# First conditioning vector from four 2 MB transfers, with x transposed meanwhile and kept in SBUF

## The reference

```python
c_act = jax.nn.silu(c)                                   # (1, 1024)
for i in range(2):
    mod = (c_act @ ada_w[i] + ada_b[i])[:, None, :]      # ada_w[i]: 1024 x 6144
    sh1, sc1, g1, sh2, sc2, g2 = jnp.split(mod, 6, axis=-1)
    u = x * (1.0 + sc1) + sh1                            # x: 1024 x 1024
    y = diff_attention(u, ...)                           # layer 0: q, k, v = u @ w_qkv, 8 heads
    x = _layer_norm(ALPHA * x + (1.0 + g1) * y, ...)     # the residual is ALPHA * x
    ...                                                  # MLP, again with a residual
```

## Time and profile before

| | us |
|---|---|
| three runs | 3074.52, 3080.66, 3080.73 (median 3080.66) |
| the profiled execution | 3074.19 |
| span of its trace | 3072.5 |
| busy: PE / PEld / DVE / ACT / POOL | 2708.4 / 2231.9 / 1689.0 / 1184.6 / 336.0 |
| mean granted TensorE clock | 0.949 of full speed |
| last conditioning block added | 75.1 |
| first product of head 0 starts | 111.6 |
| first scores of head 0 | 146.3 |

### The profile page before, as it was taken

One profiled execution on the slowest core, in us unless ns is written; L12 is line 12 of the kernel. 1 busy time (PEld: TensorE's weight loads), 2 busy tenths in 40 slices (PEclk: granted clock), 3 DMA queues, 4 the chain that ended last, 5 costly groups with the idle time before them and its releaser, 6 DMA issues.

```text
span 3072.5 us, 37975 instructions
## 1 busy us (share of the span) xinstructions
PE 2708.4 (88%) x12716; PEld 2231.9 (73%) x12716; DVE 1689.0 (55%) x2888; ACT 1184.6 (39%) x2125; POOL 336.0 (11%) x362
## 2 busy tenths in 40 slices
PE   1678878887999999999998788888789999999996
PEld 1566666665778888888776677777567888888884
DVE  3466666665575444354375777777558323232346
ACT  0355555554262120312255565665426212131223
POOL 2000000000020001016032322222101000000000
PEclk9789998886999999999999999999899999999997
DMA  6422222223434324142233111111353211111122
GB/s 195 143 68 73 70 69 66 64 59 145 150 95 130 103 69 135 44 129 61 71 115 86 21 32 27 27 32 26 128 159 86 77 48 48 48 48 48 48 82 76
DMA packets 331200, 245.78 MB, mean 80 GB/s; under 512 B 41000, under 2 KB 303447, under 8 KB 331103
## 3 DMA queue, kind: packets, MB, share of 16 engines
q1 hardware_dynamic: 314062, 185.82, 20.7%
q0 software_dynamic: 17040, 58.73, 6.3%
HBM read 215.12 MB, written 33.59 MB: 81 GB/s over the span
## 4 chain that ended last, share of the span: by engine, by line
PE 63%; DVE 13%; ACT 10%; issue 9%; DMA 4%; ACTq 0%; DVEq 0%; POOL 0%; SPq 0%; POOLq 0%
PE PA L1651 31%; PE SC L1651 24%; PE VB L1739 3%; DVE H L1184 2%; DVE soft L1566 2%; ACT H L729 2%; ACT X L745 2%; DMA ada<-in_ada_w 1%; DVE W L1102 1%; ACT X L1028 1%; ACT W L683 1%; PE TB L1658 1%; DVE H L1223 1%; ACT H L723 1%; DVE X L1588 1%
## 5 line engine op out<-in xcount | busy, mean ns | idle before, releaser
L1651 PE MATMUL PA<-U,W 128*128 128x512 f32 x3840 | 948.8, 402 | 80.8 <-DVE W L1102 46.9
L1651 PEld LDWEIGHTS PA<-U,W 128*128 128x128 f32 x3840 | 730.6, 192 | 245.5 <-issue 57.7
L683 ACT ACTIVATE W<-raw 128x1024 fp32r<-128x1024 f32 (+2 forms) x262 | 259.8, 992 | 830.9 <-PE PA L1651 389.9
L1651 PE MATMUL SC<-U,W 128*128 128x512 f32 x2064 | 484.2, 394 | 4.4 <-DVE W L1102 4.2
L1651 PEld LDWEIGHTS SC<-U,W 128*128 128x128 f32 x2064 | 389.5, 189 | 91.5 <-DVE W L1102 5.9
L1102 DVE TENSOR_TENSOR W<-raw,W 128x1024 fp32r<-128x1024 f32 (+2 forms) x262 | 313.8, 1198 | 99.6 <-ACT W L683 97.9
L1651 PE MATMUL PA<-H,W 128*128 128x512 f32 x1536 | 358.7, 393 | 3.2 <-DVE W L1102 3.2
L1651 PE MATMUL SC<-H,W 128*128 128x512 f32 x1536 | 354.4, 390 | 0.0
L1651 PEld LDWEIGHTS PA<-H,W 128*128 128x128 f32 x1536 | 288.6, 189 | 64.3 <-DVE W L1102 3.6
L1651 PEld LDWEIGHTS SC<-H,W 128*128 128x128 f32 x1536 | 288.5, 188 | 60.5 <-issue 1.0
L729 ACT ACTIVATE H<-TB 128x512 fp32r<-128x512 f32 (+3 forms) x216 | 107.8, 499 | 217.0 <-PE TB L1658 215.6
(11 more groups left out here) (209 smaller groups left out, 2984.1 us busy)
## 6 DMA issues: line engine op xcount, KB each, us to landing
raw<-in_ffn_w SPq DMA_DIRECT2D x160, 512.0 KB, 4.1
ada<-in_ada_w POOLq DMA_DIRECT2D x96, 512.0 KB, 4.7
U<-attention_out SPq DMA_DIRECT2D x4, 3584.0 KB, 17.4
raw<-in_da_w_qkv SPq DMA_DIRECT2D x24, 512.0 KB, 4.2
attention_out<-ostage SPq DMA_DIRECT2D x32, 256.0 KB, 2.7
raw<-in_da_w_o SPq DMA_DIRECT2D x16, 512.0 KB, 4.1
X<-residual SPq DMA_DIRECT2D x4, 2048.0 KB, 11.6
attention_out<-ostage SPq DMA_DIRECT2D x64, 128.0 KB, 2.3
```

The costliest lines, as they stand in the source:

```text
L683: nc.scalar.activation(W[:, slot, 0, 0:kt * P], raw[:, slot, 0:kt * P], ACT.Copy).then_inc(w_hi, 1)
L1651: ins = mm(bank, W[:, slot, a, kt * P:(kt + 1) * P], moving(b, kt)[:, cols], start=kt == first and (a, b) == SPLIT[0], stop=kt == last and ...
```

## The change

1. Scratch that lies under tensors not yet in use: `xin` (x by rows, 32 KB a partition) and `brow` (the bias table) lie where `U` will be, `ada0` (64 KB a partition) where `H` will be. So nothing of `x` waits for the bias table any more.
2. `ada_w[0][:, 0:2048]` comes in four transfers of 2 MB, issued by ACT as its first instructions, each with rows of 8 KB. DVE makes eight products of 128x2048 into `acc0` (the place of `ada`); PE adds over the partitions with 16 products after the last of them, DVE adds the bias vector once.
3. PE transposes `x` as soon as it has landed. ACT scales each half tile into `X[:, t]` (ALPHA * x), and SP stores the residual from there, in eight transfers of 512 KB.
4. ACT makes `U[:, 0]` straight from `X` with scale (1 + sc1) / ALPHA and bias sh1; DVE makes `u` from `X` in `tmp` and subtracts. The order of the half tiles is now half 0 of all t, then half 1.
5. Pieces 0 and 1 of head 0 are multiplied tile by tile as `x_lo` counts up, and `split_hi`/`split_lo` of slab 1 come earlier: `split_lo` of slabs 0 and 1 stands in DVE's program between the fifth and the sixth of the eight products.
6. POOL waits for the four transfers before it spreads the bias table, and loads the bias of head 0 (into `X[:, 4]`) only when all of `x_lo` is done.

```diff
+        with nc.sbuf_tensor("x_rows", [P, KT, S], F32) as xin, nc.sbuf_tensor("bias_row", [P, KT * S], F32) as brow:
+            pass
         U = sb("U", [P, 2, KT, S], F32R)
         X = sb("X", [P, KT, S])
+        with nc.sbuf_tensor("ada_first", [P, KT, 2 * S], F32) as ada0:
+            pass
         H = sb("H", [P, 16 * S], F32R)
...
@@ sync
             x_rows(0)
+            x_rows(1)
...
             sp.dma_start(bias_d, bvec).then_inc(bvec_out, 16)
-            sp.wait_ge(bvec_out, 16)
-            x_rows(1)
-
-            for n in range(KT * NH):
-                t, hf = n // NH, n % NH
-                sp.wait_ge(x_z, n + 1)
-                sp.dma_start(z_d[t, :, hf * HALF:(hf + 1) * HALF], tmp[:, 2 + n % 2, :]).then_inc(z_out[n % 2], 16)
+            for t in range(KT):
+                sp.wait_ge(x_z, NH * (t + 1))
+                sp.dma_start(z_d[t, :, :], X[:, t, :]).then_inc(z_out, 16)
@@ gpsimd
-            ada_loads(0, 0, 0)
-            with pool.Fori(1, 4) as b:
-                ada_loads(0, b, b)
+            for u in range(KT // 2):
+                pool.wait_ge(ada0_in[u], 16)
...
-            pool.wait_ge(xt, KT * NH)
+            pool.wait_ge(z_out, 16 * KT)
+            pool.wait_ge(x_lo, KT * NH)
             bias_load(0, 0, 0)
@@ scalar
+            for u in range(KT // 2):
+                act.dma_start(ada0[:, 2 * u:2 * u + 2, :],
+                              ada_w[0].rearrange("(t p) n -> p t n", p=P)[:, 2 * u:2 * u + 2, 0:2 * S]).then_inc(ada0_in[u], 16)
...
-            split_hi(0, 0, KT, None, 0)
             for n in range(KT * NH):
...
                 act.wait_ge(xt, n + 1)
-                act.wait_ge(x_u, n + 1)
-                nc.scalar.activation(U[:, 0, t, cols], tmp[:, n % 2, :], ACT.Copy).then_inc(x_hi, 1)
-                if n >= 2:
-                    act.wait_ge(z_out[n % 2], 16 * (n // 2))
-                nc.scalar.activation(tmp[:, 2 + n % 2, :], bank[:, 0:HALF], ACT.Copy, scale=ALPHA).then_inc(x_z, 1)
+                nc.scalar.activation(X[:, t, half(hf)], dense_bank[n % 4], ACT.Copy, scale=ALPHA).then_inc(x_z, 1)
+            split_hi(0, 0, KT, None, 0)
+            split_hi(1, 0, KT, None, 0)
+
+            act.wait_ge(aff_set, 1)
+            for n in range(KT * NH):
+                t, hf = n % KT, n // KT
+                nc.scalar.activation(U[:, 0, t, half(hf)], X[:, t, half(hf)], ACT.Identity, scale=aff[:, A_G, t:t + 1],
+                                     bias=modv(0, 0)[:, t:t + 1]).then_inc(x_hi, 1)
@@ vector
             for t in range(KT):
-                ada_mac(0, t)
-            mod_add(0, block_cols(0, 0))
-            with dve.Fori(1, 4) as b:
-                for t in range(KT):
-                    ada_mac(b, t)
-                mod_add(b, block_cols(0, b))
+                dve.wait_ge(ada0_in[t // 2], 16)
+                if t == 0:
+                    ins = nc.vector.tensor_scalar(acc0, ada0[:, t, :], cact[:, t:t + 1], None, ALU.mult)
+                else:
+                    dve.wait_ge(ada_macs, 4 * t)
+                    ins = nc.vector.scalar_tensor_tensor(acc0, ada0[:, t, :], cact[:, t:t + 1], acc0, ALU.mult, ALU.add)
+                ins.then_inc(ada_macs, 4)
+                if t == 4:
+                    split_lo(0, 0, KT)
+                    split_lo(1, 0, KT)
...
+            def x_full(n):
+                t, cols = n % KT, half(n // KT)
+                if n >= 2:
+                    dve.wait_ge(x_lo, n - 1)
+                own(nc.vector.tensor_scalar(tmp[:, n % 2, :], X[:, t, cols], aff[:, A_G, t:t + 1], modv(0, 0)[:, t:t + 1],
+                                            ALU.mult, ALU.add))
+
+            dve.wait_ge(x_z, KT * NH)
+            x_full(0)
+            for n in range(KT * NH):
+                if n + 1 < KT * NH:
+                    x_full(n + 1)
                 dve.wait_ge(x_hi, n + 1)
+                t, cols = n % KT, half(n // KT)
                 nc.vector.tensor_tensor(U[:, 1, t, cols], tmp[:, n % 2, :], U[:, 0, t, cols].bitcast(F32),
                                         ALU.subtract).then_inc(x_lo, 1)
@@ tensor
-            mod_block(0)
-            with pe.Fori(1, 4) as b:
-                pe.wait_ge(mod_done, b)
-                mod_block(b)
             for n in range(KT * NH):
...
                 for q in range(4):
-                    ins = transpose_to(bank[:, q * P:(q + 1) * P], X[:, 4 * hf + q, t * P:(t + 1) * P])
+                    ins = transpose_to(dense_bank[n % 4][:, q * P:(q + 1) * P], xin[:, 4 * hf + q, t * P:(t + 1) * P])
                 ins.then_inc(xt, 1)
+
+            pe.wait_ge(ada_macs, 32)
+            for k in range(16):
+                ins = mm(VB[:, HALF - 16 + k:HALF - 15 + k], acc0[:, k * P:(k + 1) * P], ones[:, 0:1], start=True, stop=True)
+            ins.then_inc(modp, 4)
...
-            pe.wait_ge(x_lo, KT * NH)
             pe.wait_ge(x_z, KT * NH)
-            for piece in range(6):
+            for n0 in range(NH):
+                pe.wait_ge(w_lo, 1)
+                for kt in range(KT):
+                    pe.wait_ge(x_lo, KT * n0 + kt + 1)
+                    ins = product(PA[n0][:, :], 0, u_tile, half(n0), (kt,), 0, KT - 1)
+                ins.then_inc(a0["pj_ready"], 1)
+            for piece in range(2, 6):
```

More of the change, by code:

```diff
@@ L178, in encoder @@
         osq, oraw, orstd, ofin = (X[:, 7, i * PAIR:(i + 1) * PAIR] for i in range(4))
-        bvec = X[0:HEADS0, 6:8, :].rearrange("p a s -> p (a s)")[:, 0:bias_d.shape[1]]
+        bvec = brow[0:HEADS0, 0:bias_d.shape[1]]
+        acc0 = ada[:, :, :, :].rearrange("p a b n -> p (a b n)")
         vT1 = X[:, 5, :]
@@ L228, in encoder @@
         bias_in = [sem("bias_in0"), sem("bias_in1")]; bias_masked = sem("bias_masked")
-        xt = sem("xt"); x_u = sem("x_u"); x_hi = sem("x_hi"); x_z = sem("x_z"); x_lo = sem("x_lo")
-        z_out = [sem("z_out0"), sem("z_out1")]; z_in = [sem("z_in0"), sem("z_in1")]; zs_out = [sem("zs_out0"), sem("zs_out1")]
+        xt = sem("xt"); ada0_in = [sem(f"ada0_in{u}") for u in range(KT // 2)]; aff_set = sem("aff_set"); x_hi = sem("x_hi"); x_z = sem("x_z"); x_lo = sem("x_lo")
+        z_out = sem("z_out"); z_in = [sem("z_in0"), sem("z_in1")]; zs_out = [sem("zs_out0"), sem("zs_out1")]
         ln_s = sem("ln_s"); ln_mu = sem("ln_mu"); ln_d = sem("ln_d"); ln_q = [sem("ln_q0"), sem("ln_q1")]; ln_a = [sem("ln_a0"), sem("ln_a1")]
@@ L318, in x_rows @@
             def x_rows(k):
-                sp.dma_start(X[:, 4 * k:4 * k + 4, :],
+                sp.dma_start(xin[:, 4 * k:4 * k + 4, :],
                              x[0, k * HALF:(k + 1) * HALF, :].rearrange("(t p) d -> p t d", p=P))\
@@ L521, in ada_loads @@
                 for u in range(KT // 2):
-                    if not (isinstance(nb, int) and 4 * nb + u < 2):
-                        pool.wait_ge(ada_macs, 8 * nb + 2 * u - 2)
+                    pool.wait_ge(ada_macs, 8 * nb + 2 * u - 2)
                     pool.dma_start(ada[:, u % 2, :, :],
@@ L551, in _ @@
             pool.wait_ge(ones_set, 1)
-            pool.wait_ge(xt, KT * NH)
+            pool.wait_ge(z_out, 16 * KT)
+            pool.wait_ge(x_lo, KT * NH)
             bias_load(0, 0, 0)
+            pool.wait_ge(modp, 4)
             def heads0(h0, i, last=False):
@@ L818, in _ @@
             split_hi(2, 0, KT, a0["pj_ready"], 2)
+            act.wait_ge(z_out, 16 * KT)
             for piece in range(2, 6):
@@ L1108, in ada_mac @@
                 if t % 2 == 0:
-                    dve.wait_ge(ada_in[slot], 32 * nb + 16 * (t // 4) + 16)
+                    dve.wait_ge(ada_in[slot], 32 * (nb - 4) + 16 * (t // 4) + 16)
                 src, by = ada[:, slot, t % 2, :], cact[:, t:t + 1]
@@ L1152, in _ @@
             for t in range(KT):
-                ada_mac(0, t)
-            mod_add(0, block_cols(0, 0))
-            with dve.Fori(1, 4) as b:
-                for t in range(KT):
-                    ada_mac(b, t)
-                mod_add(b, block_cols(0, b))
-            dve.wait_ge(mod_done, 4)
-            own(nc.vector.tensor_scalar(aff[:, A_G, :], modv(0, 1), 1.0, None, ALU.add))
-            own(nc.vector.tensor_scalar(aff[:, A_SUB, 0:1], vec[:, 72:73], 1.0 - LAM_INIT, None, ALU.mult))
@@ L1162, in _ @@
-            split_lo(0, 0, KT)
-            def x_lo_half(n):
-                t, cols = n // NH, slice(n % NH * HALF, (n % NH + 1) * HALF)
+                dve.wait_ge(ada0_in[t // 2], 16)
[4 more added lines that the diff above has]
+                    ins = nc.vector.scalar_tensor_tensor(acc0, ada0[:, t, :], cact[:, t:t + 1], acc0, ALU.mult, ALU.add)
@@ new lines, in _ @@
+                ins.then_inc(ada_macs, 4)
+                if t == 4:
+                    split_lo(0, 0, KT)
+                    split_lo(1, 0, KT)
+            own(nc.vector.tensor_scalar(aff[:, A_SUB, 0:1], vec[:, 72:73], 1.0 - LAM_INIT, None, ALU.mult))
+            dve.wait_ge(modp, 4)
```

(18 more changed lines are left out.)

3 lines of the change are left out of this document (removed).

## The result

The changed kernel takes 3034.72 us (median of 4 runs, 3025.05 to 3037.47) beside 3077.59 for the kernel before (4 runs). The ratio is 0.9871, with a 95% interval of 0.9847 to 0.9895; a later comparison on another occasion gave 0.9895 (0.9869 to 0.9921). (Ratios with an interval are estimates over the runs, not quotients of the two medians, which here is 0.9861.) It is faster, by 1.3% and clear of the noise, as forecast. The profiled execution took 3037.47, with a span of 3035.8: 36.7 us less than the span before, where the prediction's sum had 32.9.

The account below looks back on a forecast made before the run. Before head 0's scores, waits for conditioning weights (38.6% of the chain) and residual stores (15.1%) were taken as the bound. 3074.2 - 32.9 = 3041.3 us, median placed at 3045 between two run levels; likeliest 3036 to 3053, range 3032 to 3062.

Parts of the forecast that it names:

- the prediction's sum: Work ahead of head 0's first scores: pieces 2 to 5 end at 113.4 us against 146.3, 32.9 us less.

Follow-up runs that it names:

- run 8: Changed kernel with DVE's two weight splits moved behind the eighth product and 30 identity transposes filling PE's gap before the sums; first scores at 97.33 us, against 107.69.
- run 6: Changed kernel with the two splits behind the eighth product and the 2 MB transfers issued after SP's small loads landed; first scores at 96.1 us, against 107.69.

## What to carry to other kernels

Transfers are slow here because their destination is not free: scratch under tensors that aren't yet in use turned a latency-bound stream into one at the engines' full rate, and with small transfers nearly as well as with large ones (387 and some 410 GB/s). Look at what stands between two ready instructions in an in-order engine: two splits of 1.2 us each, put where their input was late, held back three products whose data had landed, and cost 8.2 us of a stage of 108. Check a clock column against a duration of the same instruction before trusting it, and decide by row sizes, or by the order of the issues, who gets the DMA engines when two queues are full.

## What the runs showed of the hardware

- The granted clock is shown as 1.00 before its first recorded change, while the durations are those of half clock: 128x128 fp32 transposes 0.21 us apart, against 0.11 later.
- Dense transposes alone brought the full clock, at 38.0 us (changed kernel) and at about 41 us (run 8) after starting at 35.4 and 35.8, by the durations; 2.5 us without work before the sums (run 6) were followed by a clock of 0.57 and then 0.50 in the sums, where it stayed to their end.
- Two DMA queues that are both full moved equal numbers of packets (530 and 524, 295 and 296), nearly each of them a row (1088 packets for the 1024 rows of the weights), and so shared by row size: 8 KB rows beside 4 KB rows got twice the bytes (4.08 and 1.97 million), and small loads issued from 1.3 us on landed at 25.5 beside 8 KB rows and at 13.1 beside 2 KB rows.
- 16 issues of 512 KB held ACT's sequencer for 25.8 us, four of 2 MB for 2.2: an engine that computes should issue few and large, or late.
